# Last expert's rows placed by products, router work in rows of 256, and one turn moved a piece earlier: a two-layer hybrid backbone on one core

## The reference, cut to what matters

```python
def _moe(h, router_w, w_gate, w_up, w_down):
    logits = (h @ router_w).astype(jnp.float32)
    top_v, top_i = lax.top_k(logits, TOP_K)
    top_w = jax.nn.softmax(top_v, axis=-1)
    gates = jnp.einsum('btk,btke->bte', top_w, jax.nn.one_hot(top_i, N_EXPERTS, dtype=jnp.float32)).astype(h.dtype)
    out = jnp.zeros_like(h)
    for e in range(N_EXPERTS):
        out = out + gates[..., e:e + 1] * _swiglu(h, w_gate[e], w_up[e], w_down[e])
    return out
...
    h2 = _modulate(_rms_norm(x, norm_g[2]), sh2, sc2)
    x = x + g2 * _rms_norm(ffn(h2), norm_g[3])
```

## Time and profile before

| | us |
|---|---|
| median of 3 runs | 1794.22 (1792.67 to 1799.24) |
| the profiled execution | 1796.12, span 1794.5 |
| PE busy | 1683.5 (94%) |
| DVE busy | 1052.4 (59%) |
| ACT busy | 939.5 (52%) |
| DMA, mean over the span | 238 GB/s |
| router and first gather | about 978 to 1005 |
| experts 0 to 7 | about 1005 to 1770 |
| after the last product | 1770 to 1794.5 |

### The profile page before, as it was taken

The page is one execution under the profiler, slowest core; times in us unless marked ns, Lnnn a source line. Parts: engine busy times, 40 slices in busy tenths (PEclk is TensorE's granted clock), DMA queues, the critical chain, the costliest instruction groups (busy, mean ns, idle before and its releaser), DMA issues.

```text
span 1794.5 us, 22961 instructions
## 1 busy us (share of the span) xinstructions
PE 1683.5 (94%) x8528; PEld 1337.4 (75%) x8528; DVE 1052.4 (59%) x1331; ACT 939.5 (52%) x1341; POOL 39.1 (2%) x61
## 2 busy tenths in 40 slices
PE   6898999899999999969978899999999999999995
PEld 3685458768888878648848787878787878878784
DVE  2351231333222233264274798989898989989894
ACT  3512332442222232352265577777777777777774
POOL 0000000021000000000000100000000000000000
PEclk8898999889999999979998899999999999999997
DMA  7523374389332222112204699999999999999971
GB/s 307 182 94 148 138 273 169 119 315 399 120 103 94 94 87 101 70 62 94 94 1 184 268 420 356 388 351 407 350 393 357 385 365 377 374 373 382 356 300 60
DMA packets 66890, 426.78 MB, mean 238 GB/s; under 512 B 8704, under 2 KB 11520, under 8 KB 18944
## 3 DMA queue, kind: packets, MB, share of 16 engines
q1 hardware_dynamic: 58896, 396.93, 58.2%
q0 software_dynamic: 7920, 28.84, 4.2%
HBM read 401.62 MB, written 24.12 MB: 237 GB/s over the span
## 4 chain that ended last, share of the span: by engine, by line
PE 87%; DVE 4%; ACT 4%; DMA 2%; issue 2%; SPq 0%; DVEq 0%; ACTq 0%; POOLq 0%; POOL 0%
PE ps L1504 24%; PE ps L1506 24%; PE ps L1505 24%; PE ps L1546 2%; PE ps L1522 2%; PE ps L1660 1%; DMA raw<-in_w 1%; PE ps L1555 1%; PE ps L1904 1%; PE ps L1709 1%; PE ps L1691 1%; ACT raw L508 1%; DMA cst<-in_cst 1%; DVE small L1136 1%; PE ps L1707 1%
## 5 line engine op out<-in xcount | busy, mean ns | idle before, releaser
L1371 DVE TENSOR_TENSOR wl<-raw,wh 128x1024 fp32r<-128x1024 f32 x522 | 616.1, 1221 | 74.2 <-ACT wh L853 67.4
L853 ACT ACTIVATE wh<-raw 128x1024 fp32r<-128x1024 f32 x522 | 523.7, 1053 | 109.4 <-PE ps L1506 109.4
L1504 PE MATMUL ps<-ah,wh 128*128 128x512 f32 (+1 forms) x848 | 303.5, 358 | 16.6 <-DVE al L964 9.2
L1504 PE MATMUL ps<-wh,ah 128*128 128x512 f32 (+1 forms) x800 | 308.7, 386 | 0.0
L1506 PE MATMUL ps<-wh,al 128*128 128x512 f32 (+1 forms) x800 | 302.1, 378 | 0.0
L1505 PE MATMUL ps<-wl,ah 128*128 128x512 f32 (+1 forms) x800 | 301.7, 377 | 0.0
L1505 PE MATMUL ps<-al,wh 128*128 128x512 f32 (+1 forms) x848 | 295.2, 348 | 0.0
L1506 PE MATMUL ps<-ah,wl 128*128 128x512 f32 (+1 forms) x848 | 295.1, 348 | 0.0
L934 DVE TENSOR_TENSOR wl<-raw,wh 128x1024 fp32r<-128x1024 f32 x120 | 141.5, 1221 | 101.2 <-ACT wh L465 101.2
L1504 PEld LDWEIGHTS ps<-ah,wh 128*128 128x128 f32 x848 | 162.6, 192 | 44.5 <-issue 10.1
L1505 PEld LDWEIGHTS ps<-al,wh 128*128 128x128 f32 x848 | 163.1, 192 | 20.7 <-issue 1.2
(11 more groups left out here) (241 smaller groups left out, 1600.0 us busy)
## 6 DMA issues: line engine op xcount, KB each, us to landing
raw<-in_w SPq DMA_DIRECT2D x372, 1024.0 KB, 6.5
sent<-raw POOLq DMA_DIRECT2D x16, 512.0 KB, 20.2
back<-raw POOLq DMA_DIRECT2D x16, 512.0 KB, 21.7
back<-x POOLq DMA_DIRECT2D x8, 512.0 KB
x<-sent POOLq DMA_DIRECT2D x7, 512.0 KB, 10.6
x<-in_x SPq DMA_DIRECT2D x1, 2048.0 KB, 11.6
raw<-in_ukv SPq DMA_DIRECT2D x1, 1024.0 KB, 6.6
out<-x SPq DMA_DIRECT2D x8, 128.0 KB, 2.1
```

What stands on the lines that cost most here:

```text
L853: act.activation(wh[:, J % SPLITS, piece_half(h)], slot(J % SLOTS)[:, piece_half(h)], ACT.Copy).then_inc(w_hi, 1)
L1371: ins = dve.tensor_tensor(wl[:, J % SPLITS, piece_half(h)], slot(J % SLOTS)[:, piece_half(h)], wh[:, J % SPLITS, piece_half(h)].bitcast(F3 ...
L1504: pe.matmul(out, lh, rh, start=start, stop=False)
```

## The change

1. `TURN`: group 9 is turned after q = 26, not q = 27, in the loop and in the last expert. The turn at q = 26 waits for `hT_lo` of group 8.
2. Router: the sums of squares are made for all partitions at once (ones stationary, 256 columns of `sq` moving, as in the other norms), the logits with the router stationary and 256 tokens moving (output 8x256). The inverse root is then taken on 128x256; DVE scales the 8x256 logits; PE turns them and two columns of the inverse root with small products; DVE adds the shift.
3. `sel` is made after two of the four `tok` rows; `cnt` is made earlier; `value_load` of `cnt` is moved ahead of the experts on ACT, DVE, POOL and PE.
4. `back_sel` (128 x 128 for each half of the tokens, the gate of expert 7 where a token has a row there) is made by DVE before the experts, transposed by PE and copied by DVE at the start of expert 0. After the last expert PE multiplies it with `y` in four products of 128x512, and DVE adds them to the sum of the other rows. Expert 7's rows are not written to DRAM.
5. All four indirect fetches are issued under the last expert, and DVE weighs and adds the rows (`sum_rows`) there.
6. At the end ACT scales the lower 512 columns and DVE the upper; the residual is added in 16 pieces of 128x128, and SP stores 4 pieces of 256 KB.

```diff
-TURN[GATHER] = 9
+TURN[GATHER - 1] = 9
...
+OUT_BANKS, TURN_BANKS = (0, 1, 2, 6), (3, 4, 5, 7)
...
 @block.sync
-            for k in range(KD):
-                sp.wait_ge(sem("out_ready"), k + 1)
-                sp.dma_start(out_d[:, k, :], x[:, k, 0:TL]).then_inc(sem("stored"), 16)
+            for n in range(4):
+                t, at = n // 2, 4 * (n % 2)
+                sp.wait_ge(sem("out_ready"), 4 * n + 4)
+                sp.dma_start(out_d[:, at:at + 4, t * P:(t + 1) * P], x[:, at:at + 4, t * P:(t + 1) * P]).then_inc(sem("stored"), 16)
...
 @block.scalar
-            act.activation(tok_rinv, ps[:, 4, 0:2], ACT.Ln, bias=eps[:, 0:1], scale=1.0 / D).then_inc(root_ready, 1)
...
+            root(N_O2)
...
-                act.activation(last_row[:, t, :], last_row[:, t, :], ACT.Copy, scale=out_rinv[:, t:t + 1]).then_inc(sem("y_ss"), 1)
+                act.activation(last_row[:, t, 0:512], last_row[:, t, 0:512], ACT.Copy, scale=out_rinv[:, t:t + 1]).then_inc(sem("y_norm"), 1)
...
 @block.vector
-            for t in range(2):
-                ins = dve.scalar_tensor_tensor(out=L[:, t, :], in0=ps[:, 5, 8 * t:8 * t + 8], scalar=tok_rinv[:, t:t + 1],
-                                               in1=shift_logits, op0=ALU.mult, op1=ALU.add)
+            dve.tensor_tensor(logit_rows, ps[0:NE, 5, 0:TL], rinv[0:NE, 0:TL], ALU.mult).then_inc(sem("logit_rows"), 1)
+            dve.wait_ge(sem("logits_T"), 1)
+            link(dve.tensor_tensor(L, ps[:, 6, 0:16].rearrange("p (t e) -> p t e", t=2), shift_logits[:, None, :].broadcast_to([P, 2, NE]), ALU.add))
...
+            for t in range(2):
+                ins = dve.tensor_scalar(back_sel[:, t, :], iota, rank[:, t, NE - 1:NE], -1.0, ALU.subtract, ALU.is_equal)
+            link(ins)
+            for t in range(2):
+                ins = dve.tensor_scalar(back_sel[:, t, :], back_sel[:, t, :], ex[:, t, NE - 1:NE], None, ALU.mult)
+            ins.then_inc(sem("back_sel"), 1)
...
+            def sum_rows(count):
+                dve.wait_ge(sem("gates_ready"), 1)
+                dve.wait_ge(sem("rows_back"), 16 * 4 * count)
+                for t in range(2):
+                    dve.tensor_scalar(first_row[:, t, :], first_row[:, t, :], gate_first[:, t:t + 1], None, ALU.mult
+                                      ).then_inc(sem("rows_summed"), 1)
+                for t in range(2):
+                    dve.wait_ge(sem("rows_summed"), summed_rows[0] + t + 1)
+                    dve.scalar_tensor_tensor(out=last_row[:, t, :], in0=last_row[:, t, :], scalar=gate_last[:, t:t + 1],
+                                             in1=first_row[:, t, :], op0=ALU.mult, op1=ALU.add).then_inc(sem("rows_summed"), 1)
...
+                if not no:
+                    dve.wait_ge(sem("back_sel_ps"), 1)
+                    dve.tensor_copy(back_sel_T, ps[:, 2, 0:TL]).then_inc(sem("back_sel_T"), 1)
...
                 body(NE - 1, LAST_ORDER, LAST_TURN)
+                if not no:
+                    sum_rows(1)
...
             with dve.If(most > P):
...
+            dve.memset(small[:, 0:1], 0.0).then_inc(sem("rows_final"), 1)
             for t in range(2):
+                for h in range(2):
+                    dve.wait_ge(sem("y_ps"), 2 * t + h + 1)
+                    cols = slice(512 * h, 512 * h + 512)
+                    dve.tensor_tensor(last_row[:, t, cols], last_row[:, t, cols], ps[:, OUT_BANKS[2 * t + h], :], ALU.add
+                                      ).then_inc(sem("y_sum"), 1)
+            for t in range(2):
+                dve.wait_ge(sem("y_root"), 2 * t + 2)
+                dve.tensor_scalar(last_row[:, t, 512:D], last_row[:, t, 512:D], out_rinv[:, t:t + 1], None, ALU.mult
+                                  ).then_inc(sem("y_norm_hi"), 1)
+            for t in range(2):
+                tk = slice(t * P, (t + 1) * P)
+                for k in range(KD):
+                    dve.wait_ge(sem("y_turned"), 2 * t + k // 4 + 1)
+                    dve.scalar_tensor_tensor(out=x[:, k, tk], in0=ps[:, TURN_BANKS[2 * t + k // 4], (k % 4) * P:(k % 4 + 1) * P],
+                                             scalar=scl[:, 1, 3, k, 0:1], in1=x[:, k, tk], op0=ALU.mult, op1=ALU.add
+                                             ).then_inc(sem("out_ready"), 1)
...
 @block.gpsimd
-                pool.wait_ge(w_lo, MAIN + at.J + PIECES - SLOTS + 1)
-                for t in range(2):
-                    pool.indirect_dma_start(first_row[:, t, :], None, back[:, :], rows(t)).then_inc(sem("first_rows"), 16)
+                pool.wait_ge(w_lo, MAIN + at.J + PIECES - SLOTS + 2)
+                fetch_rows()
+
+            def fetch_rows():
+                for c in range(4):
+                    pool.indirect_dma_start((first_row, last_row)[c // 2][:, c % 2, :], None, back[:, :], rows(c)
+                                            ).then_inc(sem("rows_back"), 16)
...
-                keep(NE - 1)
...
 @block.tensor
             for k in range(KD):
+                sum_square(N_O2, k)
                 pe.wait_ge(sem("x_scaled"), k + 1)
-                for t in range(2):
-                    mm = pe.matmul(ps[:, 5, 8 * t:8 * t + 8], scaled_x[:, k, t * P:(t + 1) * P], router[:, k, :],
+                mm = pe.matmul(ps[0:NE, 5, 0:TL], router[:, k, :], scaled_x[:, k, :], start=(k == 0), stop=(k == KD - 1))
...
+            pe.wait_ge(rinv_ready, ROOT_AT[N_O2] + 1)
+            for t in range(2):
+                pe.matmul(ps[:, 6, 16 + t:17 + t], rinv[0:1, t * P:(t + 1) * P], ident[0:1, 0:1], start=True, stop=True)
+            pe.wait_ge(sem("logit_rows"), 1)
+            for t in range(2):
+                mm = pe.matmul(ps[:, 6, 8 * t:8 * t + 8], logit_rows[:, t * P:(t + 1) * P], ident[0:NE, 0:NE], start=True, stop=True)
+            mm.then_inc(sem("logits_T"), 1)
...
-                            if q >= GATHER:
+                            if q >= GATHER - 1:
                                 pe.wait_ge(sem("hT_lo"), 11 * e + (at.turned + (g or 11)))
...
+            pe.wait_ge(sem("rows_final"), 1)
+            pe.wait_ge(sem("y_ready"), NE + 1)
+            pe.wait_ge(sem("y_rest"), 1)
             for t in range(2):
-                pe.wait_ge(sem("y_ss"), 2 * t + 2)
+                for h in range(2):
+                    pe.matmul(ps[:, OUT_BANKS[2 * t + h], :], back_sel_T[:, t * P:(t + 1) * P], y[:, 2 * h:2 * h + 2, :], start=True, stop=True
+                              ).then_inc(sem("y_ps"), 1)
```

More of the change, by code:

```diff
@@ L830, in _ @@
             first_split(2)
+            act.wait_ge(sem("count_ready"), 1)
+            most = act.value_load(cnt[0:1, 0:1], min_val=0, max_val=TL)
             def first_gathered():
@@ L1317, in _, with tokens @@
             dve.wait_ge(sem("tok_ps"), 1)
-            for t, h in tok_parts:
+            dve.wait_ge(sem("tok_rinv"), 1)
+            def tokens(t, h):
                 dve.scalar_tensor_tensor(out=tok[:, t, 512 * h:512 * h + 512], in0=ps[:, 2 * t + h, :], scalar=tok_rinv[:, t:t + 1],
@@ L1321, in _ @@
                                          ).then_inc(sem("tok_f32"), 1)
+            for t, h in tok_parts[0:2]:
+                tokens(t, h)
             dve.wait_ge(sem("rank_ps"), 1)
@@ L1326, in _ @@
             ins.then_inc(sem("sel_ready"), 1)
+            for t, h in tok_parts[2:4]:
+                tokens(t, h)
+            dve.wait_ge(sem("rank_ps"), 2)
+            dve.tensor_reduce(cnt[:, :], ps[:, 5, 32:40], AX.X, ALU.max).then_inc(sem("count_ready"), 1)
             dve.wait_ge(sem("ex_ready"), 2)
@@ L1416, in _ @@
             experts(0)
-            dve.wait_ge(sem("count_ready"), 1)
-            most = dve.value_load(cnt[0:1, 0:1], min_val=0, max_val=TL)
             with dve.If(most > P):
+                dve.memset(back_sel_T, 0.0).then_inc(sem("back_sel_T"), 1)
                 experts(1)
-                dve.wait_ge(sem("first_rows"), 16 * 4)
-            dve.wait_ge(sem("gates_ready"), 1)
+                sum_rows(3)
+            dve.wait_ge(sem("back_sel_T"), 1)
+            dve.memset(small[:, 0:1], 0.0).then_inc(sem("rows_final"), 1)
@@ L1431, in _ @@
-            for k in range(KD):
-                dve.wait_ge(sem("y_turned"), k // 2 + 1)
-                dve.scalar_tensor_tensor(out=x[:, k, 0:TL], in0=ps[:, k // 2, (k % 2) * TL:(k % 2 + 1) * TL],
-                                         scalar=scl[:, 1, 3, k, 0:1], in1=x[:, k, 0:TL], op0=ALU.mult, op1=ALU.add
-                                         ).then_inc(sem("out_ready"), 1)
+                for h in range(2):
[3 more added lines that the diff above has]
+                                      ).then_inc(sem("y_sum"), 1)
@@ L1455, in _, with keep @@
             pool.wait_ge(sem("rows_moved"), 16 * SENT)
+            def keep(e, at):
+                pool.wait_ge(sem("y_ready"), e + (at.done + 2))
+                pool.dma_start(back[bass.ds(SLOTS_OF * e + P * at.no, P), :].rearrange("s (a f) -> s a f", a=4), y
```

(13 more changed lines are left out.)

70 lines of the change are left out of this document (28 added, 42 removed).

## The result

The changed kernel takes 1775.92 us, the median of 4 runs (1775.24 to 1777.26). The kernel before took 1796.73 beside it (4 runs, 1792.67 to 1802.37). The ratio is 0.9883, 95% interval 0.9852 to 0.9914: 21 us faster. The profiled execution took 1775.63 us, its span is 1774.1 against 1794.5.

The account below looks back on a forecast made before the run. PE, busy 94% of the span, was taken to set the pace, so only its idle time and the tail could be won: 12.6 + 1.2 + 1.5 + 6.3 = 21.6 us, 1796.1 to 1774.5 profiled (1772.6 from the median), range 1764 to 1783.

Parts of the forecast that it names:

- Loop: Expert loop: turning group 9 earlier ends PE's wait for `sl`, 1.8 us in each of seven turns, 12.6 us.
- Rival (b): Loop gives its gain back, DVE late elsewhere or DMA unable to follow: 1785 if all lost, 1779 if half; chance 0.14.
- rival (c): Slower: the turn at q = 26 waits for `hidden(9)` and `sl` of group 8, over 3.9 us each for 1803; chance 0.03.
- Last expert: In the last expert the turn of group 10 loses its wait of 1.18 us: 1.2 us won.
- Router: Router up to the first gate-and-up: wider products let the clock return, less added DVE work; 1.5 us won.
- rival (a): The clock doesn't come back in the router: 5 us lost there instead of 1.5 won, 1779; chance 0.12.
- (d): More won than forecast: the `If` costs DVE little, or the clock doesn't fall before the router: 1764; chance 0.11.
- The end: After the last product: a tail of 17.3 or 19.0 us by clock level against 24.2; 6.3 us won.
- half of 3.79: DVE's 3.79 us for `value_load` and skipped `If` together, split evenly: 1.9 us for each.
- nearly the middle: Final products with `back_sel`: PE takes 1.9 us at the higher clock or 3.6 at the lower; a value between taken.
- `sum_rows`: Under the last expert on DVE: 4.0 us of work, hidden by some 0.6 us; otherwise at most 4.0 us cost.
- (e): The forecast itself holds, 1766 to 1778 us; chance 0.60.

Follow-up runs that it names:

- e1: The kernel before with only the turn of group 9 moved to after q = 26: 1781.27 us against 1795.42, ratio 0.9915.
- e3: The changed kernel with DVE's reading of the count moved to just before the expert loop: 1773.5 us (one run; kernel before 1798.02).
- e2: The changed kernel with the router's sums and logits again in products moving 1 or 8 columns: 1777.26 us, ratio to the kernel before 0.9886.
- e5: The changed kernel without the second pass over the experts and its `If` on every engine: 1774.31 us (one run; kernel before 1795.42).
- e4: The changed kernel with four unread products of 128x512 on PE between the last product and the final ones: 1773.17 us (one run; kernel before 1795.42).
- e6: The changed kernel with DVE's and ACT's `If` moved ahead of the copy of the last result: 1771.13 us (one run; kernel before 1798.02).

## Why the prediction was right, step by step

20.4 us were won between the two profiled executions, 0.8 of them ahead of the change: 19.6 against 21.6 forecast. The experts gave 0.3 more than forecast, the router 0.1 less with parts that cancel, the end 2.2 less.

- **Loop.** Right, by its mechanism. Between the gathers of 1182.23 and 1651.57 lie five turns, 93.87 us each, against 95.70: 1.83 won, forecast 1.8. The 0.1 us of new wait for `xel` did not come. e1 shows that the one edit does it all. Nothing was given back: PE waits for no work of DVE, and DMA followed at 379 GB/s. Rival (b) is out, and rival (c) too, since the turn at q = 26 waits for nothing.
- **Last expert.** The experts together won 14.1, forecast 13.8. Seven turns of 1.83 leave 1.3. e1, which has no transposes of `back_sel`, leaves 1.4, against 1.2 forecast. The transposes so took some 0.2 us once; the forecast had 0.3 to 0.5 for them, in the router's term. A difference of 0.2 is within what the stage varies by.
- **Router.** The number came out (1.5 forecast, 1.4 measured), but in part by luck: its parts are off and cancel. The clock fell 0.8 us after the router's first product and came back at 981.6, not 983, so rival (a) is out, and that part of (d) too. But a chunk takes 1.33 us at the higher level, not 1.15: a pass of 256 columns is some 0.26 us, not half of the 0.45 for 512. So the logits came 3.5 us earlier and not 4.8; the way to `L` took 1.4 more (forecast 1.3). `picked` is 1.95 earlier (3.5), the gather 3.3 (4.9). Against that the reading of the count took 1.43, not 1.9, and DVE's other added work 0.9, not 1.2: from the mask to `xel` it took 8.53 us against 7.93 before, 0.6 more and not 1.4. That DVE and ACT rather than PE end last there was right, and e3 shows it. The expectation of e2 carried the same fault: it took 4.8 us for the chunks, where 3.5 came.
- **The end.** The mechanism is right, the size isn't: 4.1 us won, 6.3 forecast. Two steps failed. First "half of 3.79" for the skipped `If`: it took 2.62, 0.7 more, and the reading, moved to the router, is the smaller part. Second "nearly the middle" between the two levels of the clock: up to the first square's data the clock was 0.50 throughout, and PE took 3.8 us for them, above the slow bound of 3.6 and 1.05 above the 2.75 taken. The two together account for about 1.8 of the 2.2 us. The size of the second is not fixed: in e2 and e3, where the clock was low for less of them, PE took 3.3 and 3.4 us. They have one cause: e5 shows that without the jump PE starts after 0.88 us and keeps its clock, e4 that with the jump, but with PE at work, the passes take 3.60 us. The square started at E + 7.97, between the E + 7.1 of the forecast for the lower level and its bound with the whole 3.8 for the `If`. From there to the end the forecast was 11.9 and the profile has 12.1 (11.6 in e2 and e3). What the single edits of the end won is not shown apart: no kernel undoes the products with `back_sel`, the fetches under the last expert or the smaller residual pieces one by one.
- **`sum_rows`** ended ahead of the copy, as forecast: DVE waits 0.65 us for PE after it.
- **The chances** of the cases taken as faster, (a), (d), (e) and half of (b), add to 0.90 and not 0.89, and the rest of (b) is 0.07 and not 0.08. Nothing hangs on it.

On the jump the forecast weighed a rule of the Trainium skill ("Runtime: NRT & Kernel Launch", "Instruction fetch mechanics"): a taken branch out of the fetched window stalls for a DMA fetch, while a register load costs some 0.2 us. The page states that figure for loads from HBM. The runs put it between the two readings: the larger part of the 3.79 us is the jump (2.62, and 2.41 in e6), in the rule's direction, but the reading, here of a value in SBUF, is 1.43 us by the gap in the router and 1.5 by e3, so the 0.2 does not carry over to it. No run here shows the fetch itself.

## What to carry to other kernels

Before an engine's queue is blamed, look what is queued ahead of the late split: a turn of two small products moved one place earlier in PE's order was worth more than the two other rewrites together. Anything that stops an engine for some microseconds without a releaser, such as a skipped branch or a value read into a register, belongs where the path does not run through that engine: under other engines' work (the branch in e6), or behind a long piece of its own (the reading in e3). Where TensorE pauses ahead of a short tail, price the tail at both levels of the clock, and ask what makes the pause: the branch on DVE cost 2.6 us itself and 1.3 to 1.8 more on TensorE.

## What the runs showed of the hardware

- A skipped `If` took 2.3 to 2.9 us on DVE (2.62 in the changed kernel, 2.31 in e4, 2.88 in e3) and 2.0 to 2.7 on ACT (2.58, 2.04 in e4, 2.71 in e2). A `value_load` took 1.43 us on DVE between short operations, and no visible time behind a piece of 2.35 us (e3).
- After the last product the granted clock was 1.00 until 1756.5 with PE still, and 0.50 from then until 1763.3, with PE busy again from 1757.47. In e2, after a pause of 3.38 us, it fell only at 1761.5, 0.5 us after PE had started again. With products in that pause (e4), or with a pause of 0.88 us (e5), the passes ran at 1.00 throughout.
- Products that move 1 or 8 columns left the clock at 0.50 for 17 us with PE busy 15 of them (e2); with 256 columns it was 0.50 from 978.3 and 1.00 from 981.6 until near 992, where PE paused.
- Half as many columns is not half the time: a pass of 512 took 0.45 us at the higher level (3.60 for eight), one of 256 about 0.26.
